# Splitting the rate work of the next head group over two chunk steps of an RWKV-7 and attention block

## The reference, cut to what matters

```python
w_log = -softplus(-(w0 + einsum('bsdr,drc->bsdc', tanh(lw), w2))) - 0.5
decay = exp(-exp(w_log))
iclr  = sigmoid(a0 + einsum('bsdr,drc->bsdc', la, a2))
...
k_d = kh * (1.0 + (a_d - 1.0) * k_a_h)
state = state * w_t + sa * (kk_t * a_t) + v_t * k_t      # per step, per direction
```

## Time and profile before

| what | us |
|---|---|
| median of 3 runs | 4442.32 |
| lowest and highest run | 4440.49 and 4455.31 |
| the profiled execution | 4457.15 |
| its span, first to last instruction | 4455.4 |
| TensorE busy in it | 4232.8 |
| VectorE busy | 1418.5 |
| ScalarE busy | 862.6 |
| GpSimd busy | 329.8 |

### The profile page before, as it was taken

How to read it: one execution, slowest core, us unless ns; L and a number is a source line. 1 busy time by engine, 2 the same in 40 slices (tenths; PEclk the granted TensorE clock), 3 DMA queues, 4 the chain that set the end, 5 groups by cost and what they waited for, 6 DMA issues and landing times.

```text
span 4455.4 us, 60613 instructions
## 1 busy us (share of the span) xinstructions
PE 4232.8 (95%) x25176; PEld 2757.8 (62%) x25176; DVE 1418.5 (32%) x3578; ACT 862.6 (19%) x2214; POOL 329.8 (7%) x274
## 2 busy tenths in 40 slices
PE   7899999999999899899999999999999999999999
PEld 3666674434444466666444444577787788788878
DVE  3565561120000556653112100323233422323342
ACT  3123221010000222222001000222232202222220
POOL 0022210000000012120000000000110000011000
PEclk9998999999999999899999999999999999999999
DMA  3001002212222101011221222111111111111111
GB/s 114 29 29 43 29 16 80 85 66 76 76 76 75 57 29 35 25 42 46 85 85 62 76 76 77 60 53 53 57 57 53 53 67 62 48 62 56 54 62 62
DMA packets 71343, 261.60 MB, mean 59 GB/s; under 512 B 7920, under 2 KB 7920, under 8 KB 70816
## 3 DMA queue, kind: packets, MB, share of 16 engines
q1 hardware_dynamic: 69168, 250.62, 16.1%
q10 hardware_dynamic: 1904, 7.11, 0.5%
HBM read 253.51 MB, written 4.19 MB: 58 GB/s over the span
## 4 chain that ended last, share of the span: by engine, by line
PE 90%; DVE 4%; ACT 2%; DVEq 2%; issue 1%; DMA 0%; ACTq 0%; SPq 0%
PE ps L2231 27%; PE ps L1417 25%; PE ps L2361 10%; PE ps L2326 4%; PE ps L1436 2%; PE ps L1520 2%; PE ps L815 2%; PE ps L1580 2%; PE ps L773 1%; PE ps L2242 1%; PE ps L2252 1%; PE ps L1539 1%; PE ps L852 1%; DVEq L1216 1%; PE ps L844 1%
## 5 line engine op out<-in xcount | busy, mean ns | idle before, releaser
L2231 PE MATMUL ps<-xT,ring 128*128 128x512 f32 x2656 | 1170.2, 600 | 18.5 <-ACT xT L2408 17.7
L2231 PEld LDWEIGHTS ps<-xT,ring 128*128 128x128 f32 x2656 | 509.0, 193 | 659.4 <-issue 656.1
L1417 PE MATMUL ps<-xT,ring 128*128 128x264 f32 (+2 forms) x3392 | 785.7, 387 | 18.3 <-DVE arena L1897 10.1
L1417 PEld LDWEIGHTS ps<-xT,ring 128*128 128x128 f32 (+1 forms) x3392 | 633.0, 190 | 135.7 <-DVE arena L1897 13.5
L2361 PE MATMUL ps<-arena,ring 128*128 128x512 f32 x1024 | 440.4, 592 | 1.9 <-issue 1.9
L2361 PEld LDWEIGHTS ps<-arena,ring 128*128 128x128 f32 x1024 | 194.2, 190 | 248.1 <-issue 248.1
L1417 PE MATMUL ps<-arena,ring 128*128 128x264 f32 (+1 forms) x1408 | 321.5, 386 | 2.5 <-DVEq L1798 2.3
L1417 PEld LDWEIGHTS ps<-arena,ring 128*128 128x128 f32 x1408 | 266.5, 191 | 47.3 <-issue 6.1
L1667 ACT ACTIVATE arena<-ps 128x264 f32<-128x264 f32 (+8 forms) x316 | 122.4, 388 | 634.4 <-PE ps L1417 549.6
L1039 ACT ACTIVATE arena<-ps 128x128 f32<-128x128 f32 (+1 forms) x268 | 103.1, 405 | 401.1 <-PE ps L2231 156.8
L2326 PE MATMUL ps<-yT,ring 128*128 128x512 f32 x384 | 167.6, 593 | 2.3 <-ACT yT L1032 2.3
(11 more groups left out here) (333 smaller groups left out, 4755.5 us busy)
## 6 DMA issues: line engine op xcount, KB each, us to landing
ring<-in_weights SPq DMA_DIRECT2D x467, 512.0 KB, 3.4
arena<-skew_dram ACTq DMA_DIRECT2D x8, 448.0 KB, 3.0
arena<-in_x SPq DMA_DIRECT2D x1, 2048.0 KB, 10.9
out_rows<-arena SPq DMA_DIRECT2D x8, 256.0 KB, 2.8
skew_dram<-arena ACTq DMA_DIRECT2D x4, 511.5 KB, 6.1
consts<-in_const SPq DMA_DIRECT2D x1, 1384.0 KB, 5.9
consts<-in_const ACTq DMA_DIRECT2D x1, 1252.0 KB, 5.6
arena<-in_buckets SPq DMA_DIRECT2D x1, 127.9 KB, 11.0
```

The lines of the kernel that those rows point to most:

```text
L1417: mm = pe.matmul(o[0:m, 0:cols.stop - cols.start], ws[:, k, 0:m], src[:, k, cols], start=k == 0, stop=k == nk - 1)
L2231: m = pe.matmul(o, w[:, k, :], src[:, k, 0:S], start=k == 0, stop=k == KD - 1)
```

## The change

The list puts the learning rates a0 and a1 into the filling of step 1, ahead of zr. The decay rates stay in step 0, ahead of zk. `rates_pe` and `rates_act` make one pair per call. `rates_act` now drains and rescales after each pair: the two Identity activations to `sig` in step 0, those to `kt` in step 1. For group 0 both pairs are still made one after the other; only on ScalarE does the order differ there, since the rescaling of `sig` comes before the tanh of a0 and a1.

```diff
--- before.py
+++ after.py
@@ -37,7 +37,7 @@
 MID = CHUNK // 2
 RING = 4
 SLOT = KD * P
-FILL = [["w0", "w1", "a0", "a1", "zk"], ["zr"], ["zv"], []]
+FILL = [["w0", "w1", "zk"], ["a0", "a1", "zr"], ["zv"], []]
 LEVELS = [2 ** i for i in range(1, 6)]
 HB = 64
 WINDOWS = (2, 4, 8, 16)
@@ -727,16 +727,15 @@
             for n in ("zk", "zr", "zv"):
                 proj(a, f"{n}@{c}", ws, xT)
 
-        def rates_pe(pe, L, c, a):
+        def rates_pe(pe, L, c, a, t):
 
             pe.wait_ge(*at("params", L * GROUPS + c))
-            for t, name in enumerate("wa"):
-                o = a.open_all([f"{name}{d}@{c}" for d in range(2)])
-                for q in (slice(0, S // 2), slice(S // 2, S)):
-                    for d in range(2):
-                        r = slice(64 * d, 64 * d + 64)
-                        m = pe.matmul(o[d][:, q], small[r, t, :], low[r, t, q], start=True, stop=True)
-                a.close_two(m)
+            o = a.open_all([f"{'wa'[t]}{d}@{c}" for d in range(2)])
+            for q in (slice(0, S // 2), slice(S // 2, S)):
+                for d in range(2):
+                    r = slice(64 * d, 64 * d + 64)
+                    m = pe.matmul(o[d][:, q], small[r, t, :], low[r, t, q], start=True, stop=True)
+            a.close_two(m)
 
         def norm_pe(pe, L, c, v):
 
@@ -919,8 +918,8 @@
                     if s == 2:
                         norm_pe(pe, L, c + 1, v)
                     for n in FILL[s]:
-                        if n == "w0":
-                            rates_pe(pe, L, c + 1, a)
+                        if n in ("w0", "a0"):
+                            rates_pe(pe, L, c + 1, a, "wa".index(n[0]))
                         if n[0] == "z":
                             proj(a, f"{n}@{c + 1}", ws[c + 1], xT)
                 for d in range(2):
@@ -969,19 +968,20 @@
             o = a.open(f"{name}@{c}")
             a.close(act.activation(zp[:, j % 2, 1:S + 1], o, ACT.Copy))
 
-        def rates_act(act, L, c, a):
+        def rates_act(act, L, c, a, t):
 
             act.wait_ge(*at("params", L * GROUPS + c))
-            for t, buf in (("w", sig), ("a", aa)):
-                for d in range(2):
-                    o = a.open(f"{t}{d}@{c}")
-                    a.close(act.activation(buf[d], o, ACT.Tanh, scale=0.5, bias=gcol(c, f"{t}0_{d}")))
+            name, buf = (("w", sig), ("a", aa))[t]
+            for d in range(2):
+                o = a.open(f"{name}{d}@{c}")
+                a.close(act.activation(buf[d], o, ACT.Tanh, scale=0.5, bias=gcol(c, f"{name}0_{d}")))
             act.drain()
             for d in range(2):
-                act.activation(sig[d], sig[d], ACT.Identity, scale=0.5, bias=0.5).then_inc(STEPS["sig"][0], 1)
-            for d in range(2):
-                act.activation(kt[d], aa[d], ACT.Identity, scale=gcol(c, "ka_half"), bias=gcol(c, "ka_rest"))\
-                   .then_inc(STEPS["kt_scale"][0], 1)
+                if t == 0:
+                    act.activation(sig[d], sig[d], ACT.Identity, scale=0.5, bias=0.5).then_inc(STEPS["sig"][0], 1)
+                else:
+                    act.activation(kt[d], aa[d], ACT.Identity, scale=gcol(c, "ka_half"), bias=gcol(c, "ka_rest"))\
+                       .then_inc(STEPS["kt_scale"][0], 1)
 
         def keys_act(act, L, c):
 
@@ -1077,8 +1077,8 @@
                     take(f"o{s - 1}", osb[:, s - 1, :], n=P)
                 if c < GROUPS - 1:
                     for n in FILL[s]:
-                        if n == "w0":
-                            rates_act(act, L, c + 1, a)
+                        if n in ("w0", "a0"):
+                            rates_act(act, L, c + 1, a, "wa".index(n[0]))
                         if n[0] == "z":
                             take_z(act, L, c + 1, a, n)
                     if s == 1:
@@ -2301,7 +2301,8 @@
                     ws[c].next()
                 proj_z(pe, L, 0, a, ws[0], proj)
                 pe.wait_ge(*at("low_ready", L, 2))
-                rates_pe(pe, L, 0, a)
+                for t in range(2):
+                    rates_pe(pe, L, 0, a, t)
                 proj(a, "u@0", ws[0], xT)
                 norm_pe(pe, L, 0, v)
                 proj(a, "aq@0", ws[0], xT)
@@ -2436,7 +2437,8 @@
                     act.wait_ge(*at("lnx", L, i))
                     act.activation(low[:, i, :], low[:, i, :], f).then_inc(STEPS["low_ready"][0], 1)
                 take_z(act, L, 0, a, "zv")
-                rates_act(act, L, 0, a)
+                for t in range(2):
+                    rates_act(act, L, 0, a, t)
                 keys_act(act, L, 0)
                 o = a.open("u@0")
                 a.close(act.activation(up_[:, 8:8 + S], o, ACT.Copy))
```

## The result

| | us, median | lowest to highest | runs |
|---|---|---|---|
| before | 4448.8 | 4439.9 to 4464.2 | 7 |
| changed | 4424.8 | 4419.2 to 4435.6 | 7 |

The ratio is 0.9948, with a 95% interval of 0.993 to 0.9966: 0.52% faster, some 23 us. The forecast was 4437.1 with a range of 4427 to 4452, and "no change that shows".

What follows compares the result with a forecast made beforehand. TensorE, busy for 95% of the span, was taken to bound the kernel, with time won only where it idles or runs at low clock. 3.4 us (hole) + 1.8 (clock) = 5.2 off the 4442.3 median gave 4437.1, range 4427 to 4452.

Steps and rivals of the forecast that it cites:

- The hole of step 0: TensorE's 0.85 us idleness after w0, w1 in step 0, in six groups, goes: 3.4 us won, 5.1 if counted in full.
- The pair itself: The eight matmuls of a0, a1 move from step 0 to step 1, 1.06 us at full clock: net zero.
- no new wait in step 1: In step 1 TensorE meets no wait at the moved pair, zr or U; 1 us in hand for the pair's bank.
- ScalarE's queue: ScalarE gains some 2.9 us in step 1, is still idle some 6 us when zr arrives: nothing on the path.
- no table load: On ScalarE, splitting the tanh over two steps around an exponential adds no table load; the sum has none.
- group 0: In group 0 of each layer `sig` comes 1.3 us earlier, but VectorE then idles until TensorE's norm: zero gain.
- The clock: Half clock after three step 0 holes may end sooner: up to 5.3 us, or nothing or a loss; 1.8 us taken.
- Rival 1: The clock rises sooner everywhere in step 0: 8.7 us off, 4433.6; chance 0.22.
- the far form: All five step 0 half-clock stretches fall to 3.4 us: 10.2 us off besides 3.4, 4428.7; chance 0.05.
- Rival 2: Slower: half clock gets longer as everything behind step 0 shifts by 0.4 to 0.9 us: 4450.8; chance 0.12.

Runs made afterwards that it cites:

- after_hole: The changed kernel, but TensorE waits in step 0, ahead of zk, until the tanh of w0 is over: 4450.4 us, 1.0002 of the kernel before.

## Why the prediction was wrong

- **The hole of step 0** (3.4 us won): right, also in size. The waits of line 738 went from 8 to 2, and the rest of the time, over all runs, fell by 3 us. That the page's idle time fell by 3.4 us too is chance: the forecast's 3.4 us counts a hole at half clock by half, its idle time alone is 5.1 us, and at line 738 4.9 us went.
- **The pair itself** (net zero), **no new wait in step 1**, **ScalarE's queue**, **no table load**, **group 0**: right. The pair cost 0.96 us in step 1, no bracket appeared, and ScalarE idled for 1.72 us before the tanh and for 4.13 before zr. In group 0 VectorE stands idle until the norm for 3.98 us instead of 2.91, so the earlier `sig` is swallowed as foretold. Both kernels load tables 52 times, and none of the loads is at the tanh of the rates. That exp and tanh share a table set, which the Trainium skill says (ScalarE: Activation LUTs, Table sets: the hidden batching unit), holds in this trace.
- **A reading that was off, without effect**: zk was to come "up to 1.9 us earlier". At half clock the pair and the hole are 2.86 us (344.7 to 347.56 in the earlier trace rows). No term of the sum hangs on it.
- **The clock** ("I take one of the three: 1.8 us"): this is the step that failed. The term measured 20 us over all runs (227 to 186 us of half clock, the latter the mean of the changed kernel's 12 runs). It was mis-sized because it was looked for at the wrong place. I priced only the stretches of step 0, beside the edit. The largest stretches of the block, six of 10 to 13.7 us behind step 2, I took as fixed: "leave the ends of the stretches alone". I had one of them in the rows, and named TensorE's wait for ScalarE there, but asked only whether the wait's length would change. It did not; whether the clock fell behind it did. What sets that beforehand stays open.
- **Rival 1** (the clock rises sooner) had the right sign and the right kind, with 0.22, of it 0.05 for the far form at 4428.7. It too placed the gain in step 0, where 10 us of half clock went, worth 3 us of time. The Trainium skill's sentence that the throttled state is the default and activity releases it (TensorE: Matmul & The Clock Gate, What's actually happening) fits the traces (behind a wait of 2.45 us the clock fell to 1.2 GHz, and rose again after 10 to 13.7 us in which TensorE worked) but would not have told which of the waits counts.
- **Rival 2** contained the missing thought with the wrong sign: "everything behind step 0 shifts by 0.4 to 0.9 us", and the stretches vary. A shift can act either way, and the bound should have been taken over all the stretches behind the edit: six of them, up to 6.8 us each, 40 us. With that bound the range would have reached down to about 4400, and the chance of faster by over 0.3% would have been well above 0.07.
- The median of three runs was low: over 78 runs the kernel before stands at 4452, not 4442. By that luck the forecast time is off by 12 us only. The forecast change is off by more: against the same base I forecast -5 and got -23.

## What to carry to other kernels

Before costing an edit that moves work by a microsecond, list the low-clock stretches of the whole stage and the waits that open them, and treat each as a coin that the edit may turn, not as a constant. Read what a change did from the page in two numbers, the fall of idle time and the fall of busy time at the same count of instructions: the second is mostly clock, and may have nothing to do with the edit's reason. Two kernels that differ only by a harmless delay are the control for that. Removing or shortening the wait ahead of the stretch gained 27 and 28 us here in the kernel before, where the delays gained 4 at most. And look where the profiled execution lies among its runs before counting stretches in it.

## What the runs showed of the hardware that I had not expected

- The same wait of 2.45 us, behind the same matmuls, was followed by 10 to 13.7 us at half clock in 6 of 6 places of one execution, and in 2 of 6 of another, in kernels that differ by shifts of about 1 us. 8 more matmuls per group in step 1 changed the half clock of a run from 227 to 208 us in one kernel and from 182 to 210 in the other.
- Short waits can be followed by it as well: in the changed kernel all six waits of 1.40 us at line 905 in step 0 of groups 0 to 2 have half clock behind them, from 3.4 to 6.8 us; with the hole put back, four of the six have.
- The runs of a kernel lie 12 to 37 us apart where there are ten or more, and they do so mostly by their clock: among the 12 runs of after_hole the fastest (4441 us) has a mean granted clock of 0.977 and the slowest (4463 us) 0.972. Over the 78 runs of the kernel before the standard deviation of the time is 7.0 us, and that of the rest 2.8.
- What stays open is why the version with the pair in step 2 has 204 us of half clock and the changed kernel 182 to 191, at nearly the same distance between step 0 and the wait, and how much idleness in step 0 adds by itself.
